# Turning five projection chunks on VectorE, from the staging tile to their place, in a two-layer decoder trunk on one core

## The reference

```
# layer 0: xn = rmsnorm(h)
proj = xn @ w_in                       # 2048 -> 5656 columns
q_a, kv_a, g_a, q_b, k_b, v_b = split(proj)
o_a = nsa_attention(q_a, compress(kv_a[0]), compress(kv_a[1]), kv_a[2..5], sigmoid(g_a))
o_b = diff_attention(q_b, k_b, v_b)
h = h + concat(o_a, o_b) @ w_out

# layer 1: xn = rmsnorm(h)
xb, yb = split(xn @ w_in, 2)           # 2048 -> 2 * 2048 columns
y  = gelu(yb)
xc = causal_conv4(xb) + conv_b         # per channel, along the positions
r, i = sigmoid(xc @ wa + ba), sigmoid(xc @ wx + bx)      # in 8 blocks
a = exp(-8 * r * softplus(-lambda)); u = sqrt(1 - a*a) * i * xc
h = h + (scan(h_t = a_t h_{t-1} + u_t) * y) @ w_out
```

## Time and profile before

| | us |
|---|---|
| median of 3 runs | 2373.56 (2373.51 to 2375.59) |
| profiled execution, its own time | 2373.45 |
| its span | 2371.7 |
| TensorE busy | 2353.1 |
| VectorE busy | 1566.8 |
| ScalarE busy | 1143.5 |

### The profile page before, as it was taken

One profiled execution on the slowest core, in us unless ns is written; L12 is line 12 of the kernel. 1 busy time (PEld: TensorE's weight loads), 2 busy tenths in 40 slices (PEclk: granted clock), 3 DMA queues, 4 the chain that ended last, 5 costly groups with the idle time before them and its releaser, 6 DMA issues.

```text
span 2371.7 us, 29398 instructions
## 1 busy us (share of the span) xinstructions
PE 2353.1 (99%) x10768; PEld 1948.8 (82%) x10768; DVE 1566.8 (66%) x2212; ACT 1143.5 (48%) x1482; POOL 8.5 (0%) x31
## 2 busy tenths in 40 slices
PE   9999999999999999999999999999999999999998
PEld 7888778888888888888888888888888888888887
DVE  5556678676676676666597777866676676666656
ACT  5435555544444444444454575544444444444455
POOL 0000000000000000000000000000000000000000
PEclk9999999999999999999999999999999999999999
DMA  6844536666666666666568455566666666566664
GB/s 191 281 134 116 147 121 205 187 193 195 194 188 197 192 193 194 193 193 193 185 194 264 127 160 183 190 194 192 191 193 194 194 187 198 192 194 195 194 207 151
DMA packets 241195, 443.86 MB, mean 187 GB/s; under 512 B 16680, under 2 KB 30800, under 8 KB 240976
## 3 DMA queue, kind: packets, MB, share of 16 engines
q1 hardware_dynamic: 240768, 442.23, 61.1%
q10 hardware_dynamic: 336, 0.41, 0.0%
HBM read 440.49 MB, written 2.10 MB: 187 GB/s over the span
## 4 chain that ended last, share of the span: by engine, by line
PE 95%; DVE 2%; ACT 2%; issue 1%; DMA 0%; SPq 0%; ACTq 0%; DVEq 0%
PE ps L1527 30%; PE ps L1529 30%; PE ps L1528 30%; PE ps L1754 1%; PE ps L1479 1%; ACT w_hi L651 1%; DVE w_lo L949 1%; ACT prob L862 0%; DVE prob L1295 0%; PE ps L1664 0%; PE ps L1677 0%; DMA h<-in_x_dram 0%; PE ps L1659 0%; PE ps L1702 0%; ACT junk L719 0%
## 5 line engine op out<-in xcount | busy, mean ns | idle before, releaser
L949 DVE TENSOR_TENSOR w_lo<-raw,w_hi 128x1024 fp32r<-128x1024 f32 x820 | 998.5, 1220 | 738.8 <-ACT w_hi L651 733.2
L651 ACT ACTIVATE w_hi<-raw 128x1024 fp32r<-128x1024 f32 x820 | 862.8, 1055 | 1023.3 <-PE ps L1529 1002.9
L1527 PE MATMUL ps<-w_hi,xa_hi 128*128 128x512 f32 x1664 | 647.7, 389 | 0.0
L1529 PE MATMUL ps<-w_hi,xa_lo 128*128 128x512 f32 x1664 | 647.4, 389 | 0.0
L1528 PE MATMUL ps<-w_lo,xa_hi 128*128 128x512 f32 x1664 | 647.3, 389 | 0.0
L1527 PEld LDWEIGHTS ps<-w_hi,xa_hi 128*128 128x128 f32 x1664 | 312.4, 188 | 64.9
L1529 PEld LDWEIGHTS ps<-w_hi,xa_lo 128*128 128x128 f32 x1664 | 312.4, 188 | 64.8
L1528 PEld LDWEIGHTS ps<-w_lo,xa_hi 128*128 128x128 f32 x1664 | 312.4, 188 | 64.5
L1527 PE MATMUL ps<-w_hi,xb_hi 128*128 128x512 f32 x864 | 349.8, 405 | 0.2 <-DVE w_lo L949 0.2
L1529 PE MATMUL ps<-w_hi,xb_lo 128*128 128x512 f32 x864 | 337.4, 391 | 0.0
L1528 PE MATMUL ps<-w_lo,xb_hi 128*128 128x512 f32 x864 | 336.8, 390 | 0.0
(11 more groups left out here) (242 smaller groups left out, 1017.2 us busy)
## 6 DMA issues: line engine op xcount, KB each, us to landing
raw<-in_w_ffn_gate_dram SPq DMA_DIRECT2D x176, 512.0 KB, 4.4
raw<-in_w_ffn_up_dram SPq DMA_DIRECT2D x176, 512.0 KB, 4.3
raw<-in_w_ffn_down_dram SPq DMA_DIRECT2D x176, 512.0 KB, 4.6
raw<-in_w_in_attn_dram SPq DMA_DIRECT2D x88, 512.0 KB, 3.7
raw<-in_w_ple_gate_dram SPq DMA_DIRECT2D x64, 512.0 KB, 4.6
raw<-in_w_in_rec_dram SPq DMA_DIRECT2D x64, 512.0 KB, 4.1
raw<-in_w_out_attn_dram SPq DMA_DIRECT2D x32, 512.0 KB, 3.8
raw<-in_w_out_rec_dram SPq DMA_DIRECT2D x32, 512.0 KB, 3.8
```

The lines of the kernel that those rows point to most:

```text
L651: nc.scalar.activation(w_hi[:, s, 0:n], raw[:, s, 0:n], ACT.Copy).then_inc(hi_ready, 1)
L949: nc.vector.tensor_tensor(w_lo[:, s, 0:n], raw[:, s, 0:n], w_hi[:, s, 0:n].bitcast(F32), ALU.subtract).then_inc(lo_ready, 1)
L1527: nc.tensor.matmul(o, xh[:, k, tok], w_hi[:, s, wk], start=(k == 0), stop=False)
L1529: ins = nc.tensor.matmul(o, xl[:, k, tok], w_hi[:, s, wk], start=False, stop=(k == nkt - 1))
```

## The change

Five chunks (qa0, qa1, xb0, xb1 and yb2) are no longer turned by TensorE and copied by VectorE. VectorE turns them with 32x32 block transposes straight from `stage` to `qaT`, `xbT` or `yT`: `turn_in_place`, four instructions after each of four `w_lo`, 16 a chunk. For qa0, xb0, xb1 and yb2 these slots are j=4 to 7 of the next chunk. For qa1 they are j=0 to 3 of kvc, since the gates chunk behind it has only four slots. A new semaphore `placed` counts the chunks turned. Who writes `stage` next, the convolution of xb0 and xb1, and the product with yb2's part of `yT` wait for it.

```diff
+TURNED_IN_PLACE = [("qa", 0), ("qa", 1), ("xb", 0), ("xb", 1), ("yb", 2)]
...
 def banks_of(p, i, r):
 
-    return 0 if is_moved(p, i, r) else p.kinds[r].banks
+    return 0 if is_moved(p, i, r) or place_no(p, i, r) else p.kinds[r].banks
...
                         if m == 0:
                             act.wait_ge(turned, turn_no(q, i, r))
+                            if places_before(q, i, r):
+                                act.wait_ge(placed, places_before(q, i, r))
...
+            def turn_in_place(q, i, r, c):
+
+
+                dve.wait_ge(evac[q.kinds[r].evac], evac_no(q, i, r)[1])
+                col = 4 * (2 * i + r)
+                rows = slice(32 * c, 32 * c + 32)
+                src = stage[:].rearrange("p m (k d) -> p k m d", k=4)[:, :, :, 32 * c:32 * c + 32]
+                for a in range(4):
+                    o = {"qa": lambda: qaT[rows, col:col + 4, :],
+                         "xb": lambda: xbT[rows, col:col + 4, 3:3 + S],
+                         "yb": lambda: yT[rows, col:col + 4, :]}[q.name]()
+                    ins = nc.vector.transpose(
+                        o.rearrange("p k (m t) -> p k m t", m=NT)[:, :, :, 32 * a:32 * a + 32], src[32 * a:32 * a + 32])
+                if c == 3:
+                    ins.then_inc(placed, 1)
+                    if q.name == "xb":
+                        conv(2 * i + r)
...
-                if k.name == "xb":
+                if k.name == "xb" and not place_no(q, i, r):
                     conv(2 * i + r)
...
+                    if j < 4 and q.name == "gkvc" and r == 1:
+                        turn_in_place(*two_before(q, i, r), j)
                     if j == 3:
                         evacuate(*prev)
+                    if 4 <= j < 8 and place_no(*prev):
+                        turn_in_place(*prev, j - 4)
```

More of the change, by code:

```diff
@@ L178, in is_moved, with place_no, places_before @@
     return k.moved > 0 if p.loop else 2 * i + r < k.moved
+def place_no(p, i, r):
+    key = (p.name, 2 * i + r) if not p.loop else None
+    return TURNED_IN_PLACE.index(key) + 1 if key in TURNED_IN_PLACE else 0
+def places_before(p, i, r):
+    order = ("qa", "gkvc", "kvsw", "qk0", "qk1", "vb", "xb", "yb")
+    return sum((order.index(n), c) < (order.index(p.name), 2 * i + r) for n, c in TURNED_IN_PLACE)
 def banks_of(p, i, r):
-    return 0 if is_moved(p, i, r) else p.kinds[r].banks
+    return 0 if is_moved(p, i, r) or place_no(p, i, r) else p.kinds[r].banks
 def chunks_before(p, i, r):
@@ L406, in trunk @@
         dve_step = sem("dve_step")
+        placed = sem("placed")
         ple_step = sem("ple_step")
@@ L959, in evacuate @@
                     dve.wait_ge(turned, turn_no(q, i, r))
+                if kind in ("gates", "kvc", "kvs", "kvw", "xb") and places_before(q, i, r):
+                    dve.wait_ge(placed, places_before(q, i, r))
                 if q.norm is not None and kind != "ple":
@@ L1087, in conv @@
             def conv(c):
-                dve.wait_ge(turn_used, named["xb"].turn0 + 2 * c + 2)
+                i, r = divmod(c, 2)
+                if place_no(named["xb"], i, r):
+                    dve.wait_ge(placed, place_no(named["xb"], i, r))
+                else:
+                    dve.wait_ge(turn_used, turn_no(named["xb"], i, r) + 2)
                 for tap in range(4):
@@ L1428, in griffin @@
                     dve.wait_ge(r_scan, g + 1)
-                    dve.wait_ge(turn_used, named["yb"].turn0 + 2 * (g + 1))
+                    if place_no(named["yb"], *divmod(g, 2)):
+                        dve.wait_ge(placed, place_no(named["yb"], *divmod(g, 2)))
+                    else:
+                        dve.wait_ge(turn_used, turn_no(named["yb"], *divmod(g, 2)) + 2)
                     nc.vector.tensor_tensor(xc[:, t4], xbT[:, t4, 0:S], yT[:, t4], ALU.mult).then_inc(r_h, 1)
```

## The result

| | before | changed | difference |
|---|---|---|---|
| median of 10 runs each | 2373.53 us | 2381.03 us | +7.5 us |
| lowest and highest run | 2373.24 to 2375.59 | 2378.14 to 2383.0 | |
| ratio of the times | | 1.0028 (95%: 1.002 to 1.0036) | slower |
| profiled execution (span) | 2373.45 (2371.7) | 2378.21 (2376.4) | +4.76 (+4.7) |

The changed kernel is slower. Its profiled execution is one of the quickest of its ten, 2.8 us under the median. The profile thus shows most of the loss, and the experiments have to find the rest.

The account below looks back on a forecast made before the run. VectorE, not TensorE, was taken to bound the kernel at slot 15. The places sum as 5.90 + 1.38 − 0.87 − 0.6 = +5.8 us on 2373.45, giving 2379.3 us, range 2376.3 to 2382.6.

Parts of the forecast that it names:

- What bounds the kernel: At slot 15 VectorE, not TensorE, is the bound: `w_lo` starts 1.28 us before TensorE's slot, with no lead.
- What is removed: TensorE's eight transposes per block go away: 0.87 us each, 4.35 us for five.
- What is added: VectorE's four block transposes take 1.79 us, making its slot 3.05 us against TensorE's 2.73.
- The rival of slow targets: Block transposes to `qaT`, `xbT` or `yT` slower than to `sg`, 2.56 us for four: up to 2389 us; chance 6%.
- First and second place: qa0 in slots 12 to 15 and qa1 in slots 20 to 23: slot 24's second matmul +5.90 us.
- Third place: xb0 in x12 to x15: late `w_lo` makes x16 +1.38 us in place of −0.87.
- Fourth: xb1 in x20 to x23: VectorE's added work is hidden, so −0.87 us.
- Fifth: yb2 in x60 to x63: about 0.25 us of the saving is given back, so −0.6 us.
- only the first stop is real: VectorE gets 1 us ahead at slot 20, so qa1 in slots 20 to 23 costs nothing: 2377.1 us; chance 22%.
- The cover holds: VectorE has room at all five places and the saving is whole: 2369.2 us; chance 4%.
- The rival of the clock: TensorE's clock falls to 1.2 GHz in the stop before slot 15: 0 to +1.5 us; 20% to cost over 0.7.

Follow-up runs that it names:

- The softplus experiment: The changed kernel with the softplus and its argument moved from slots 14 and 15 to slots 28 and 29: 2375.03 us, ratio 1.0.
- xb0 alone: The changed kernel with only xb0 turned in place, the other four chunks as before: 2377.4 us, ratio 1.0015.
- work before x16: The changed kernel with 8 more 128x128 identity matmuls into an unused bank ahead of slot x16: 2379.55 us, ratio 1.0024.
- the last version: The changed kernel with the softplus moved to slots 28 and 29 and xb0 left to TensorE and its copies: 2371.4 us, ratio 0.9992.
- qa0 and qa1 alone: The changed kernel with only qa0 and qa1 turned in place: 2379.49 us, ratio 1.0023.
- qa0 alone: The changed kernel with only qa0 turned in place, in slots 12 to 15: 2380.75 us, ratio 1.0031.
- xb1 and yb2 alone: The changed kernel with only xb1 and yb2 turned in place: 2373.12 us, ratio 0.9995.
- both fillings before slot 15: The changed kernel with 42, or 22, more identity matmuls ahead of slot 15: 2383.24 us, ratio 1.0038, and 2379.78 us, ratio 1.0027.

## Why the prediction was right

It said slower, 2379.3 us, range 2376.3 to 2382.6. The median was 2381.03, which is slower and inside the range.

- **What bounds the kernel.** Right. The share of busy time said that VectorE had room, the lead at slot 15 said that it had none. The softplus experiment shows that this lead decided: with all 20 groups of transposes where they were, and only the softplus moved, 6.0 of 7.5 us come back (0.8 of them without the change too).
- **What is removed, 0.87 us a block.** It came back whole where `w_lo` is early: 0.90 at xb1.
- **What is added, 1.79 us for four.** Right: 1.77 to 1.80 to all three targets. The rival of slow targets (6%) is out.
- **First and second place, +5.90.** 6.24 from slot 12 on; the stop 5.18 against 5.3, `w_lo` of slot 15 +4.44 against +4.29, of slot 16 +6.37 against +6.07.
- **Third place, +1.38.** 1.51 in the profiled pair, 1.2 and 1.3 in the two clear runs of xb0 alone. (Its own terms, 1294.8 + 0.1 − 1293.55, give 1.35.) **Fourth, −0.87:** −0.90. **Fifth, −0.6:** −0.59.
- **The rival "only the first stop is real"** (22%) is out: `w_lo` of slot 20 came 5.33 us behind that of slot 16, before 5.50, which is 0.17 us sooner where the rival needed 1. **"The cover holds"** (4%) is out.
- **The rival of the clock** (20% for costing over 0.7) came true in its fall and not in its price, at its place: 1.2 GHz over slot 15, 5.23 us in place of 2.86. All of the 2.4 us hid, since without the fall slot 24 comes no sooner (39.87 against 39.69 us from slot 12). The 0.3 us by which 6.24 exceeds 5.90 are thus not the clock's; `w_lo` of slot 16 already has them. By the page that the prediction names on this, the Trainium skill's "TensorE: Matmul & The Clock Gate", section "Why this matters for your kernels", idle gaps bring the half rate back; the trace agrees, at 0.50 over slot 15.

**What was mis-sized.** The median is 1.7 us above the forecast. The profiled pair's sum without the head start is 6.26, 0.5 over the forecast's 5.8. The rest is the clock at the third place. I priced x16 by `w_lo`'s lateness and a restart of 0.1, and looked for a fall only behind the long stop. The 2 us stop at x16 can bring one too, which then costs 1.6 us more; eight useless products in the stop took the median down by 1.5 and the scatter from 4.9 to 2.1 us.

Two things more differ between executions and have nothing to do with the change: the head start, and a fall of the clock behind a stop at 340 to 347 us (last section). Together with the fall at x16 they would give the spread. From 2373.45, the sum of 6.26 gives 2379.7 us, which is where eight of the ten runs with work before x16 lie (2379.33 to 2379.9). With a fall at x16 it gives 2381.3, with the other fall as well 2382.9, and with a head start of 1.5 and no fall 2378.2. The ten runs of the changed kernel span 2378.14 to 2383.0. That the profiled execution lies 2.8 us under the median I put down to its having had the head start and neither fall; its other nine executions have no trace, so this is argued. The forecast had the sum and none of the rest. That the rest moved the median by so little that it stayed inside the range is in part luck.

**What stays open.** Why the clock falls at a stop of 2 us in one execution and not in another, and why none of the ten runs with work before x16 lies as high as the fall at 340 to 347 us would put it. And whether the last version beats the kernel before: its interval ends at 1.0001.

## What to carry to other kernels

Before giving an engine at 66% more work, read at that very place how far ahead its results are, and what else stands there in its order: 5 us of once-only work made most of the loss, and moving it alone took 6.0 of 7.5 us back. Price a stop of TensorE at its length plus the clock it may lose behind it, and ask whether another late engine hides that loss. A profile is one execution: where its time isn't the median, look for what the other runs had. And before two profiles are compared at one point, count both from a point ahead of the change.

## What the runs showed of the hardware that I had not expected

- **Behind a stop of some 2 us TensorE's clock fell to 1.2 GHz in some executions and not in others.** At x16 the stop of 1.98 us left it at 1.00 in the changed kernel's profiled execution and brought 0.50 in that with the late softplus.
- **The kernel before has such a stop too.** Ahead of a group of the attention's products, which starts at 338.60 to 347.26 us, TensorE stands 2.06 to 2.08 us in all thirteen profiled executions. The row and the window behind it of the kernel before, then the same window of the kernel with the late softplus:

```profile
340.59 0.46 PE L1702 MATMUL ps<-vb_tok,probTd 128*128 128x128 f32 x2 [2.06 <-issue]
```

```profile
342.00:344.00 2.00, 2.00 (x11) 1.67 (x10) 1.64 (x4) 1.61 (x8) 0.00 (x0) 1.00 0.38 142
```

```profile
342.00:344.00 2.00, 2.00 (x6) 1.52 (x6) 1.62 (x3) 1.32 (x8) 0.00 (x0) 0.50 0.27 103
```

  Six of the thirteen show the fall (qa0 and qa1 alone, qa0 alone, xb1 and yb2 alone, the late softplus, both fillings before slot 15), seven don't, among them before and the changed kernel. In the three of the six that leave xb0 to TensorE, slot 24 to x16 takes 1218.8 to 1218.9 us in place of 1217.2: such a fall costs 1.6 us, and it has nothing to do with the change.
- **The program's start differs by up to 2 us between executions.** In the profiled execution of the changed kernel the six identity products behind the transposes of `h`, recorded as twelve instructions, took 1.50 us, in that of before 2.49 at the lower clock:

```profile
6.84 0.66 PE L1527 MATMUL ps<-ident,h 128*128 128x128 f32 x4 [1.03 <-DMA h<-in_x_dram]
7.34 1.50 PE L1511 MATMUL ps<-ident 128*128 128x128 f32 x12
```

  The wait for `h` was 1.03 us here and 1.88 before. In the five profiled executions in which those products took 1.50 us, slot 12's `w_lo` starts at 41.14 to 41.64; in the eight in which they took 2.49 to 2.77, at 42.27 to 43.21. The kernel with work before x16 is one of the eight: its slot 24 stands at 82.48, the forecast's figure, but with a head start of 0.36 us, so that the agreement to the hundredth is luck (39.71 us from slot 12, +6.26).
- **An fp32 product of two 128x128 tiles in a row takes 0.22 us** (9.3 us for 42; 5.07 us for 22, with the last one's end), and the profile records it as two instructions.
